# Layer norm tail of a hybrid decoder layer on eight cores: statistics from centred squares, factors one tile behind, gain and store two tiles behind, seven buffers for x

## The reference

```
merged = g_c * y_conv + g_a * y_att
out = jnp.einsum('bsd,de->bse', merged, w_o)
return layer_norm(DN_ALPHA * x + out, ln_g, ln_b)     # DN_ALPHA = 2 ** 0.25

def layer_norm(x, g, b):
    mu = mean(x); var = mean(square(x - mu))          # over the 1024 channels of one token
    return (x - mu) * rsqrt(var + 1e-5) * g + b
```

## Time and profile before

| | us |
|---|---|
| median of 3 runs (lowest, highest) | 948.56 (948.48, 950.81) |
| profiled execution, its own time | 949.12 |
| span of its slowest core (core 0) | 947.4 |
| spans of the 8 cores | 944.7 to 947.4 |
| core 0: PE busy, DVE busy, ACT busy, POOL busy | 896.1, 467.8, 372.6, 74.6 |

### The profile page before, as it was taken

The page is one execution under the profiler, slowest core; times in us unless marked ns, Lnnn a source line. Parts: engine busy times, 40 slices in busy tenths (PEclk is TensorE's granted clock), DMA queues, the critical chain, the costliest instruction groups (busy, mean ns, idle before and its releaser), DMA issues.

```text
span 947.4 us, 15606 instructions; the slowest of 8 cores (944.7 to 947.4 us)
## 1 busy us (share of the span) xinstructions
PE 896.1 (95%) x5814; PEld 500.9 (53%) x5904; DVE 467.8 (49%) x682; ACT 372.6 (39%) x546; POOL 74.6 (8%) x85
## 2 busy tenths in 40 slices
PE   3999999999999999999999999999999999999980
PEld 2786765459585775555544444444444444444430
DVE  3233455745274455744675444555633333334775
ACT  0203348852655227756642222223322222222663
POOL 4000000000000000000000000000000000000554
PEclk9999999999999999999999999999999999999996
DMA  8996121111200212112141222222572222000684
GB/s 129 159 167 82 23 28 30 23 24 24 46 13 6 41 24 34 24 23 46 23 68 25 43 45 29 39 40 31 93 171 39 39 40 39 1 1 23 205 255 162
DMA packets 21641, 55.81 MB, mean 59 GB/s; under 512 B 1728, under 2 KB 9920, under 8 KB 21184
## 3 DMA queue, kind: packets, MB, share of 16 engines
q0 software_dynamic: 16528, 36.97, 26.6%
q1 hardware_dynamic: 5040, 17.85, 5.9%
HBM read 83.39 MB, written 8.39 MB: 97 GB/s over the span
## 4 chain that ended last, share of the span: by engine, by line
PE 87%; DMA 4%; ACT 3%; issue 3%; DVE 2%; POOL 1%; POOLq 0%; DVEq 0%; SPq 0%; ACTq 0%
PE pp L414 80%; PE pp L607 4%; PE pp L579 3%; DMA xt<-xtok 2%; DMA xO<-xo 1%; ACT ob L811 1%; ACT junk L777 1%; DVE ys L769 1%; POOL ob L826 1%; DVE sd L790 0%; DVE ob L821 0%; ACT PT L585 0%; ACT Uacc L635 0%; ACT sa L784 0%; POOLq L102 0%
## 5 line engine op out<-in xcount | busy, mean ns | idle before, releaser
L414 PE MATMUL pp<-xO,wr 128*128 128x512 bf16 x2363 | 530.4, 379 | 5.4 <-issue 2.4
L414 PEld LDWEIGHTS pp<-xO,wr 128*128 128x128 bf16 x2432 | 234.8, 98 | 280.6 <-issue 4.2
L585 ACT ACTIVATE PT<-pp 128x1024 bf16<-128x1024 f32 x96 | 93.0, 1021 | 95.4 <-PE pp L579 86.7
L414 PE MATMUL pp<-wr,xO 128*128 128x256 bf16 x768 | 88.5, 277 | 15.9 <-DMA xO<-xo 15.9
L414 PEld LDWEIGHTS pp<-wr,xO 128*128 128x128 bf16 x768 | 81.5, 120 | 21.9 <-issue 16.0
L432 DVE CAST V<-pp 128x512 bf16<-128x512 f32 (+1 forms) x70 | 47.8, 683 | 91.5 <-PE pp L414 91.4
L334 POOL DMA_DIRECT2D wr<-ws x54 | 29.0, 537 | 756.5 <-PE pp L414 599.5
L739 DVE TENSOR_TENSOR mS<-pp,gcS 128x512 f32<-128x512 f32 x32 | 22.1, 691 | 116.1 <-PE pp L414 116.1
L628 DVE TENSOR_TENSOR Uacc<-Uacc,pp 128x512 f32<-128x512 f32 x64 | 52.9, 869 | 51.9 <-PE pp L607 51.6
L594 DVE TENSOR_TENSOR PT<-PT,mk_bf 128x1024 bf16<-128x1024 bf16 x96 | 65.4, 691 | 25.5 <-ACT PT L585 23.5
L448 ACT ACTIVATE KT<-pp 128x512 bf16<-128x512 f32 x72 | 41.5, 583 | 76.0 <-PE pp L414 75.8
(11 more groups left out here) (55 smaller groups left out, 663.1 us busy)
## 6 DMA issues: line engine op xcount, KB each, us to landing
wr<-ws POOLq DMA_DIRECT2D x42, 512.0 KB, 6.0
xt<-xtok SPq DMA_DIRECT2D x16, 512.0 KB, 6.5
out<-ob SPq DMA_DIRECT2D x15, 512.0 KB, 3.9
xO<-xo POOLq DMA_DIRECT2D x4, 1024.0 KB, 27.3
xH<-xh POOLq DMA_DIRECT2D x4, 1024.0 KB, 57.1
wr<-ws POOLq DMA_DIRECT2D x8, 384.0 KB, 6.0
wo<-wo POOLq DMA_DIRECT2D x2, 1024.0 KB, 19.7
wr<-ws POOLq DMA_DIRECT2D x4, 256.0 KB, 3.9
```

What stands on the lines that cost most here:

```text
L414: inst = e.matmul(ps[bank][:, c0:c0 + n], lhs[k], rhs[k], start=(k == 0), stop=(k == len(lhs) - 1))
L585: S.add("act", lambda e: e.activation(out=PT[h][:, :], in_=pp[h][:, :], func=AF.Exp), writes=[("PT", h)], banks=[2 * h, 2 * h + 1])
```

## The change

The arithmetic of the norm is written another way, the work of a tile is spread over three iterations in place of two, and x by tokens gets seven buffers.

- Buffers: `xt` grows from three to seven, over memory that the convolution is done with; `ys` 0 to 2 move to memory of the merge's inputs (`aT3`, `uT0`, `uT1`), free after the merge's last matmul.
- Loads: tiles 0 to 6 are handed to SP ahead of the merge; the load of tile t+7 follows `residual(t)` in iteration t, waits for it, and stands ahead of the stores of later tiles.
- Statistics: `centre(t)` (a small DVE instruction) makes minus the mean right after `residual(t)`. ACT squares y with that as its bias, so that the accumulator holds the sum of centred squares, and takes the root behind it, with no DVE instruction between the two.
- Order in iteration t: `project(t)`, `residual(t)`, load, `centre(t)`, `spread(t)`, `factors(t-1)`, `normalise(t-1)`, `gain(t-2)`, `shift_out(t-2)`.
- Last tile: ACT copies the shift into `pp[1]`. `residual` and uncentred `squares` stay in halves; three small DVE instructions and a root follow; then each half is (y + minus mean) * gain and (that) * factor + shift, all four passes on DVE. The first half is stored from ACT's queue, the second from SP's.

```diff
+        NXT = 7
+        xt = [at(f"xt{i}", o_t + 8192 + 4096 * i, [128, DM], F32) for i in range(NXT)]
+        ys = [at(f"ys{i}", o_xh + 4096 * i, [128, DM], F32) for i in range(3)]
...
+        for t in range(NXT):
+            load_xt(t)
         it = 0
         for j in range(8):
...
+        def centre(t):
+            small(t, 4, sd[t % 6][:, 0:1], -1.0 / DM, ALU.mult, None, ALU.bypass, [("sd", t % 6, 0)])
+        def spread(t):
+            S.add("act", lambda e: e.activation(out=junk[:, :], in_=ys[iy][:, :], func=AF.Square, bias=sd[i6][:, 4:5],
+                                                accum_out=sa[i6][:, 1:2]),
+            S.add("act", lambda e: e.activation(out=sa[i6][:, 2:3], in_=sa[i6][:, 1:2], func=AF.Sqrt, scale=1.0 / DM, bias=cst[:, 40:41]),
...
+        def centred_gain(t, c0, n):
+            S.add("dve", lambda e: e.scalar_tensor_tensor(out=ob[i3][:, c0:c0 + n], in0=ys[iy][:, c0:c0 + n], scalar=sd[i6][:, 4:5],
+                                                          in1=pp[3][:, c0:c0 + n], op0=ALU.add, op1=ALU.mult),
+        def scaled_out(t, c0, n):
+            S.add("dve", lambda e: e.scalar_tensor_tensor(out=ob[i3][:, c0:c0 + n], in0=ob[i3][:, c0:c0 + n], scalar=sd[i6][:, 2:3],
+                                                          in1=pp[1][:, c0:c0 + n], op0=ALU.mult, op1=ALU.add),
+            store(t, c0, n, "act" if c0 == 0 else "sp")
...
         for t in range(last):
-            if t + 2 <= last:
-                load_xt(t + 2)
-            if t >= 1:
-                factors(t - 1)
-                normalise(t - 1, 0, DM)
             for hf in range(2):
                 project(t, hf)
             residual(t, 0, DM, 0)
-            squares(t, 0, DM, 1)
+            if t + NXT <= last:
+                load_xt(t + NXT)
+            centre(t)
+            spread(t)
             if t >= 1:
-                gain(t - 1, 0, DM)
-                shift_out(t - 1, 0, DM)
-            spread(t)
+                factors(t - 1)
+                normalise(t - 1)
+            if t >= 2:
+                gain(t - 2)
+                shift_out(t - 2)
...
         project(t, 0)
         project(t, 1)
+        S.add("act", lambda e: e.activation(out=pp[1][:, :], in_=gb[:, DM:2 * DM], func=AF.Copy), reads=["gb"], writes=["gbq"], banks=[2, 3])
         residual(t, 0, 512, 0)
         squares(t, 0, 512, 0)
-        gain(t - 1, 0, DM)
-        shift_out(t - 1, 0, DM)
-        residual(t, 512, 512, 4)
+        factors(t - 1)
+        normalise(t - 1)
+        gain(t - 2)
+        shift_out(t - 2)
+        residual(t, 512, 512, 1)
         squares(t, 512, 512, 1)
...
+        S.add("act", lambda e: e.activation(out=a[:, 2:3], in_=a[:, 1:2], func=AF.Sqrt, bias=d[:, 6:7]),
+        gain(t - 1)
+        shift_out(t - 1)
+        centred_gain(t, 0, 512)
+        centred_gain(t, 512, 512)
+        inverse(t)
+        scaled_out(t, 0, 512)
+        scaled_out(t, 512, 512)
```

More of the change, by code:

```diff
@@ L302, in build @@
         S.over([(k, i) for k in ("gcS", "gaS", "mS") for i in range(2)] + ["wo0", "wo1", ("wr", 5)], n_att)
-        S.over(["gb"] + [("xt", i) for i in range(3)] + [("ys", i, c0) for i in range(3) for c0 in (0, 512)], n_conv)
+        S.over(["gb"] + [("xt", i) for i in range(NXT)], n_conv)
+        S.over([("ys", i, c0) for i in range(3) for c0 in (0, 512)],
+               [("aT", 3, h, m) for h in range(2) for m in range(4)] + [("uT", cc, w) for cc in range(2) for w in range(4)])
         S.over([("ys", 3, 0), ("ys", 3, 512), ("junk", 0, 0), ("junk", 0, 512)] + [("ob", i, c0) for i in range(3) for c0 in (0, 512)]
@@ L766, in residual @@
         def residual(t, c0, n, k):
-            i3, iy, i6, pb = t % 3, t % 4, t % 6, t % 3
+            ix, iy, i6, pb = t % NXT, t % 4, t % 6, t % 3
             S.add("dve", lambda e: e.scalar_tensor_tensor(
-                out=ys[iy][:, c0:c0 + n], in0=xt[i3][:, c0:c0 + n], scalar=ALPHA, in1=pp[pb][:, c0:c0 + n],
+                out=ys[iy][:, c0:c0 + n], in0=xt[ix][:, c0:c0 + n], scalar=ALPHA, in1=pp[pb][:, c0:c0 + n],
                 op0=ALU.mult, op1=ALU.add, accum_out=sd[i6][:, k:k + 1]),
-                reads=[("xt", i3)], writes=halves("ys", iy, c0, n) + [("sd", i6, k)], banks=[2 * pb + i for i in range(2) if 512 * i < c0 + n and c0 < 512 * i + 512])
+                reads=[("xt", ix)], writes=halves("ys", iy, c0, n) + [("sd", i6, k)], banks=[2 * pb + i for i in range(2) if 512 * i < c0 + n and c0 < 512 * i + 512])
@@ new lines, in small @@
+        def small(t, o, i, s1, op0, s2, op1, extra=()):
+            i6 = t % 6
+            S.add("dve", lambda e: e.tensor_scalar(out=sd[i6][:, o:o + 1], in0=i, scalar1=s1, scalar2=s2, op0=op0, op1=op1),
+                  reads=list(extra), writes=[("sd", i6, o)])
+        def centre(t):
+            small(t, 4, sd[t % 6][:, 0:1], -1.0 / DM, ALU.mult, None, ALU.bypass, [("sd", t % 6, 0)])
+        def spread(t):
+            iy, i6 = t % 4, t % 6
+            S.add("act", lambda e: e.activation(out=junk[:, :], in_=ys[iy][:, :], func=AF.Square, bias=sd[i6][:, 4:5],
+                                                accum_out=sa[i6][:, 1:2]),
+                  reads=halves("ys", iy, 0, DM) + [("sd", i6, 4)], writes=halves("junk", 0, 0, DM) + [("sa", i6, 1)])
+            S.add("act", lambda e: e.activation(out=sa[i6][:, 2:3], in_=sa[i6][:, 1:2], func=AF.Sqrt, scale=1.0 / DM, bias=cst[:, 40:41]),
+                  reads=[("sa", i6, 1), "cst"], writes=[("sa", i6, 2)])
@@ L783, in root @@
             i6 = t % 6
[L784 to L788, removed]
+            S.add("dve", lambda e: e.reciprocal(out=sd[i6][:, 2:3], in_=sa[i6][:, 2:3]),
+                  reads=[("sa", i6, 2)], writes=[("sd", i6, 2)])
@@ L789, in small, with factors @@
+        def factors(t):
             i6 = t % 6
[L790 to L805, removed]
@@ L807, in normalise @@
-        def normalise(t, c0, n, eng="act"):
-            i3, iy, i6 = t % 3, t % 4, t % 6
[L809 to L817, removed]
@@ L819, in gain, with normalise @@
-        def gain(t, c0, n):
+            inverse(t)
+            small(t, 3, sd[i6][:, 4:5], sd[i6][:, 2:3], ALU.mult, None, ALU.bypass, [("sd", i6, 4), ("sd", i6, 2)])
+        def normalise(t):
+            i3, iy, i6 = t % 3, t % 4, t % 6
+            S.add("act", lambda e: e.activation(out=ob[i3][:, :], in_=ys[iy][:, :], func=AF.Identity,
+                                                scale=sd[i6][:, 2:3], bias=sd[i6][:, 3:4]),
+                  reads=halves("ys", iy, 0, DM) + [("sd", i6, 2), ("sd", i6, 3)], writes=halves("ob", i3, 0, DM))
@@ L820, in gain @@
+        def gain(t):
             i3 = t % 3
-            S.add("dve", lambda e: e.tensor_tensor(out=ob[i3][:, c0:c0 + n], in0=ob[i3][:, c0:c0 + n], in1=pp[3][:, c0:c0 + n], op=ALU.mult),
-                  reads=halves("ob", i3, c0, n) + ["gbp"], writes=halves("ob", i3, c0, n), banks=[6, 7])
-        def shift_out(t, c0, n, eng="pool"):
+            S.add("dve", lambda e: e.tensor_tensor(out=ob[i3][:, :], in0=ob[i3][:, :], in1=pp[3][:, :], op=ALU.mult),
+                  reads=halves("ob", i3, 0, DM) + ["gbp"], writes=halves("ob", i3, 0, DM), banks=[6, 7])
```

46 lines of the change are left out of this document (21 added, 25 removed).

## The result

| | before | after |
|---|---|---|
| median (lowest to highest), us | 948.72 (948.48 to 950.81) | 937.23 (936.99 to 937.55) |
| profiled execution, us | 949.12 | 937.43 |
| span of the slowest core | 947.4 (core 0) | 935.9 (core 3) |

The ratio is 0.9878, with a 95% interval of 0.9866 to 0.9889: 11.5 us faster, where 8.2 were forecast. 937.23 lies under the range of 938.2 to 943.8.

A forecast was written before the change was run, and what follows sets the result against it. TensorE bounds the kernel up to the tail, there a loop through ACT and DVE. Core 7: tile 14 at 920.5 + landing 15.4 + end 3.1 + lag 0.3 = 939.3, giving 940.4 us predicted; range 938.2 to 943.8.

The forecast's parts named there:

- The forecast case: Whole kernel: the norm in the tail follows TensorE at 3.45 us per tile, time 940.4 us, chance 0.60.
- Loop: Norm in the tail: the loop through ACT and DVE within a tile goes, pace from 4.00 to 3.45 us per tile.
- DVE's list: VectorE's work per tile in the tail: sum 3.1 us, bounds 3.1 and 4.0, taken as 3.1 to 3.2.
- squares with a bias operand: ScalarE pass per tile in the tail, bias read per partition: between 1.06 and 1.24 us, taken as 1.15.
- the ring: Three `ob` buffers in the tail: they bound the pace only if stores take above 5.2 us to land.
- the 4.00 us per tile of before: Norm's pace in the old kernel's tail on core 7, read from 872.13 to 932.16 in 15 tiles.
- Loads: Loads of x: 7 of 16 go ahead of the merge at no cost; in the tail no residual waits for x.
- The lag of 0.3 us at tile 14: Tail transfers: tiles 2 to 8 ask 304 GB/s against 279 seen, leaving 0.3 us late (between 0 and 2).
- stores behind loads: Rival, SP's queue in the tail: stores land after 6.7 us, pace 3.96 in tiles 2 to 8, 942 to 943.7; chance 0.18.
- Tile 14: Tail on core 7: tile 14 starts 14 x 3.45 us after tile 0, at 920.5 instead of 928.23, 7.8 us saved.
- The end, up to the landing: Last tile, from tile 14's residual: last store issued at 11.9 us, landed at 15.4 (between 13.8 and 16.5).
- The end, from the landing: After the last store lands: the old kernel's 3.1 us to the end of the span stay.

## Why the prediction was too careful

The forecast case came about: the norm follows TensorE. Step by step, on the slowest core (core 3 in place of the assumed core 7):

- *Loop.* Right. Pace 3.45 predicted, 3.453 measured. DVE's list 3.05 (3.1 to 3.2 taken), squares with a bias operand 1.15 (taken: 1.15), no wait for the ring on core 3; where stores took 4.5 and more L817 waited a little, as the prediction's working had it. Taken apart, it is the order that does it (6.2 us), not the statistics (0.0). One reading was loose: the 4.00 us per tile of before is 3.84 to 3.93 from tile 1 on and 5.28 in the first, with the table load. The sum is none the worse, as it counts from tile 0 to tile 14 as a whole.
- *Loads.* Right that none waits for x and that the early ones cost nothing; TensorE has no idle in the merge. The lag of 0.3 us at tile 14 did not come: where 304 GB/s were asked, stretches of 5 us reached up to 341 (core 5), above the 279 that I had for an upper rate. That was a mean over 10 us and no limit; the earlier trace rows already had 338 in one us. The 358 GB/s of the Trainium skill (DMA: Bandwidth & Descriptors, section Bandwidth) would have served better. Over 5 us the trace stays under it; over a single us it goes above, to 397 GB/s (core 3, 932 to 933 us, at the end, where only stores run), so it is no ceiling for short stretches. The rival "stores behind loads" falls with it: stores land after 3.0 to 4.5 us at the median, not 6.7. What the prediction did not say is how much the loads carry once the loop is gone: 6.3 us.
- *Tile 14.* 920.5 predicted, 919.43 measured on core 3. 0.8 us of this is where the slowest core begins: its projection starts at 868.2 in the one trace that I had and at 867.4 here (tile 0 at 872.13 and 871.36), and at 867.4 and 868.0 in the two repeats. 0.28 is that the residual of tile 0 starts 0.28 us later after its matmuls than the others do (871.36 to 874.53 is 3.17, not 3.45); I had counted 14 full tiles from it.
- *The end, up to the landing.* Last issue 11.9 after tile 14's residual, predicted 11.9. No more bytes move after 15.3, predicted 15.4; the landing event, a later mark, comes at 15.7. Right.
- *The end, from the landing.* This is the step that failed: "From landing to the end of the span 947.1 - 944.0 = 3.1 stay." 1.2 stayed (by the landing event 0.7 of 2.7). The 3.1 was no property of the stores: it was the rest of GpSimd's 5.47 us. Measured from GpSimd's last instruction the end is the same in before and after, and since the change takes that instruction from 13.4 to 11.0 us after the residual, the tail shrinks by 2.4. I had the two rows to see it: the chain of waits ended on POOL's queue, and eight cores with eight landings offered eight tests.

3.4 us in all on the profiled span (939.3 against 935.9): 1.9 from the step behind the landing, 0.1 from the landing, 0.8 from the start, 0.3 from the lag, 0.3 from tile 0. The range was too narrow because it held bounds for the landing and none for the constant behind it.

## What to carry to other kernels

A constant at the end of a span belongs to one event: look on several cores from which one it is really constant before an edit moves any of them. Two limits can hide each other: the loads alone gave 1 us, the order without them about 2.4 (948.9 less 944.05 less the 2.4 of the last tile), both together 8.8 (948.9 less 937.7 less 2.4); to price one, put the other right first. Here a loop that crossed two engines within a tile was undone by taking each step from the tile before; the price was a buffer held longer, and transfers that then had to keep up.

## What the runs showed of the hardware

- GpSimd reaches the closing barrier 5.28 us after the end of its last instruction, for a pass of 2.35 us as for one of 0.19 us, on every core of every run in which nothing else was later. In the others (all cores without GpSimd at the end, two cores without the copy) the span ended 0.29 us after the last landing. A kernel that ends on GpSimd work pays for it unless something else ends later still.
- TensorE's granted clock fell to 0.81 for 15.1 us while it was busy without a gap and 300 GB/s of transfers ran: a level of its own, neither full nor half, with matmuls 0.26 us apart in place of 0.215 (first run with the old last tile, core 4). On another chip in another hour the same code kept 1.00. What triggers it is not shown.
- The table load ahead of the first root of the tail took 1.28 us in both kernels. It cost time only under the old order, where the next residual stood behind that root.
- A ScalarE pass over 1024 elements took 1.06 us with no operand per partition, 1.15 with one and 1.24 with two. The Trainium skill, ScalarE: Activation LUTs, section What ACT_TABLE_LOAD costs, gives 93 ns for each; the trace agrees.
